# Mixing the two softmax maps two places behind the logits instead of one, with a deeper second buffer, in the second attention stage

## The reference

```python
def diff_mixer(h, rel_bias, w_in, lam_q1, ..., w_out, lambda_init):
    ...
    def block(args):
        ...
        logits = jnp.einsum('bqmd,blmd->bmql', qb, k).astype(jnp.float32)
        logits = logits + jnp.moveaxis(bias, -1, 0)[None]
        logits = jnp.where((rel >= 0)[None, None], logits, -jnp.inf)
        p = jax.nn.softmax(logits, axis=-1).reshape(bsz, B_HEADS, 2, BLOCK_Q, L)
        a = p[:, :, 0] - lam * p[:, :, 1]
        return jnp.einsum('bhql,blhe->bqhe', a.astype(v.dtype), v)
    ...
    o = rms_norm(o, subln_g) * (1.0 - lambda_init)
    return (o * jax.nn.silu(gate)) @ w_out
```

## Time and profile before

| | |
|---|---|
| median of 3 runs | 3884.29 us (3883.88 to 3887.35) |
| the profiled execution, its own time | 3887.83 us |
| its span | 3886.0 us |
| PE busy | 3448.4 us, 89% |
| DVE busy | 2143.9 us, 55% |
| ACT busy | 2016.0 us, 52% |
| GpSimd busy | 524.2 us, 13% |

### The profile page before, as it was taken

One profiled execution on the slowest core, in us unless ns is written; L12 is line 12 of the kernel. 1 busy time (PEld: TensorE's weight loads), 2 busy tenths in 40 slices (PEclk: granted clock), 3 DMA queues, 4 the chain that ended last, 5 costly groups with the idle time before them and its releaser, 6 DMA issues. The chain is left out here.

```text
span 3886.0 us, 65323 instructions
## 1 busy us (share of the span) xinstructions
PE 3448.4 (89%) x18786; PEld 2575.8 (66%) x18786; DVE 2143.9 (55%) x5870; ACT 2016.0 (52%) x3490; POOL 524.2 (13%) x550
## 2 busy tenths in 40 slices
PE   6869798878999999996975999999978899889699
PEld 3746454466666666664855888889956666666587
DVE  3659799995555556554644111000077777777344
ACT  2548689965777777774224111111156666666222
POOL 2000255101111111110211111111020000000011
PEclk7989899977999999998987999999989999999799
DMA  8651677663233222324532444322142222220342
GB/s 231 181 135 33 194 224 230 182 211 103 80 83 81 79 75 81 83 76 138 173 135 93 117 122 118 92 70 68 57 127 69 72 69 72 69 69 30 134 140 98
DMA packets 428415, 436.41 MB, mean 112 GB/s; under 512 B 81697, under 2 KB 341185, under 8 KB 427457
## 3 DMA queue, kind: packets, MB, share of 16 engines
q1 hardware_dynamic: 417440, 430.93, 37.4%
q10 hardware_dynamic: 10784, 3.18, 0.8%
HBM read 271.44 MB, written 162.53 MB: 112 GB/s over the span
## 5 line engine op out<-in xcount | busy, mean ns | idle before, releaser
L1253 DVE CUSTOM_DVE_ANT_0 a_att_sb_lg<-a_att_ps_s,mask 128x512 f32<-128x512 f32 (+3 forms) x512 | 302.0, 595 | 220.5 <-PE a_att_ps_s L1144 179.6
L1150 PE MATMUL b_att_ps_s<-b_att_sb_k,b_att_sb_q 64*128 64x512 f32 (+3 forms) x1920 | 295.2, 418 | 84.7 <-DVE b_att_sb_lg L1255 64.0
L1327 ACT ACTIVATE a_att_sb_pT<-a_att_ps_t 128x512 f32<-128x512 f32 (+3 forms) x640 | 316.0, 530 | 104.2 <-PE a_att_ps_t L1163 97.3
L1319 ACT ACTIVATE b_att_sb_lg<-b_att_sb_lg,b_att_sb_negm 128x384 f32<-128x384 f32 (+15 forms) x256 | 305.6, 1198 | 122.6 <-DVE b_att_sb_negm L1261 122.5
L1319 ACT ACTIVATE a_att_sb_lg<-a_att_sb_lg,a_att_sb_negm 128x384 f32<-128x384 f32 (+15 forms) x256 | 307.3, 1200 | 77.5 <-DVE a_att_sb_negm L1261 77.5
L1163 PE MATMUL a_att_ps_t<-ident,a_att_sb_lg 128*128 128x128 f32 x2176 | 339.8, 279 | 0.0
L1255 DVE TENSOR_SCALAR_CACHE_REDUCE b_att_sb_lg<-b_att_ps_s 128x512 f32<-128x512 f32 (+3 forms) x512 | 282.8, 590 | 95.8 <-PE b_att_ps_s L1150 80.4
L1682 DVE TENSOR_SCALAR_CACHE_REDUCE mask<-scores,threshold_bits 128x384 bf16<-128x384 f32 (+8 forms) x288 | 322.5, 1186 | 1.2
L1163 PEld LDWEIGHTS a_att_ps_t<-ident,a_att_sb_lg 128*128 128x128 f32 x2176 | 248.6, 141 | 107.4 <-issue 57.2
L1143 PE MATMUL a_att_ps_s<-a_att_sb_k,a_att_sb_q 128*128 128x512 f32 (+3 forms) x640 | 287.1, 449 | 30.9 <-DVE a_att_sb_mx L1253 16.4
L1180 PE MATMUL a_att_ps_o<-a_att_sb_pT,a_att_sb_v 128*64 128x256 f32 (+1 forms) x2304 | 297.4, 377 | 0.0
(11 more groups left out here) (282 smaller groups left out, 6896.4 us busy)
## 6 DMA issues: line engine op xcount, KB each, us to landing
a_att_sb_q<-scratch_qT SPq DMA_DIRECT2D x512, 64.0 KB, 2.5
select_sb_w_gate<-in_a_w_in SPq DMA_DIRECT2D x32, 512.0 KB, 4.9
mask_sb_mod_w<-in_mod_w SPq DMA_DIRECT2D x16, 1024.0 KB, 6.6
a_att_sb_k<-scratch_kT SPq DMA_DIRECT2D x128, 128.0 KB, 2.8
b_qkgv_sb_w<-in_b_w_in SPq DMA_DIRECT2D x32, 512.0 KB, 4.8
b_att_sb_q<-scratch_qT SPq DMA_DIRECT2D x128, 128.0 KB, 2.5
b_att_sb_k<-scratch_kT SPq DMA_DIRECT2D x64, 256.0 KB, 4.0
front_sb_mod_w<-in_mod_w SPq DMA_DIRECT2D x8, 1024.0 KB, 8.5
```

The lines of the kernel that those rows point to most:

```text
L1150: mm = nc.tensor.matmul(s_ps[:, (n + m) % SR, 0:z - a], q[rows, p // 2 % QS, x, cols], k[rows, slot, y, a:z], start=(j == 0), stop=(j == 2))
L1253: x = nc.vector.tensor_tensor_reduce(out, src, tab, 1.0, 2 * NEG, sign, ALU.max, top[:, col:col + 1])
L1319: nc.scalar.activation(buf, buf, ACT.Exp, bias=negm[:, p, m:m + 1], accum_out=sums[:, b, ds(h * M + m, 1)]).then_inc(exp_done, 1)
L1327: nc.scalar.activation(pT[:, r % 2, a:z, c:c + P], t_ps[:, n % TR, 0:z - a], ACT.Copy).then_inc(t_left, 1)
```

## The change

Four numbers and one test are different. DVE inverts and mixes block p - 2 at place p instead of block p - 1; `lg2` gets four buffers instead of two, which hold a block's second map for longer; and GpSimd prepares three early weight blocks instead of five, so that the last stage loads and splits five itself.

```diff
-EARLY_OUT = 5
+EARLY_OUT = 3
 OR = 2
 QS, OS, KPIECES = 4, 4, 4
-LR, LR2 = 4, 2
+LR, LR2 = 4, 4
...
                 if M == 2:
                     for head, x in both(h, p, before):
-                        if 1 <= x <= NB:
-                            invert(head, x - 1)
+                        if 2 <= x <= NB + 1:
+                            invert(head, x - 2)
                 if h is not None:
                     maximum(h, p)
                 for head, x in both(h, p, before):
                     for r in outputs_here(x):
                         output(head, r)
-                    if M == 2 and 1 <= x <= NB:
-                        mix(head, x - 1)
+                    if M == 2 and 2 <= x <= NB + 1:
+                        mix(head, x - 2)
```

## The result

Medians of four runs each: 3933.09 us after (3930.13 to 3936.11) against 3884.09 us before, a ratio of 1.0121 with a 95% interval of 1.0106 to 1.0136, or 49 us. 3922 was predicted, with a range of 3892 to 3960.

A forecast was written before the change was run, and what follows sets the result against it. DVE was taken to bound each head's growing part and PE the shrinking part; 25 (later mix) + 12 (clock) + 2.5 - 1.5 (early weights) = 38 us over the median of 3884.3, so 3922 us, range 3892 to 3960.

The forecast's parts named there:

- The mechanism: Second attention stage, growing part: transposes wait for the later mix, logits queue behind them, and DVE idles without PE's lead.
- two waits of 6.4 us for a mix: Kernel before: the transposes on PE were said to wait twice for a mix, 6.4 us in total.
- The main term, 25 us: Growing parts of the second attention stage: PE 3.1 us late per head by place 7, eight heads, +25 us.
- a barer loop end: DVE before place 6: a shorter mix covers less of the hardware loop's end, 0.41 us more per head.
- DVE's relief: Growing part: DVE mixes smaller blocks up to place 8, a gain of 1.87 us per head.
- The clock, 12 us: Growing parts: slow turns at 1.2 GHz now on DVE's path, 1.5 us per head, +12 us; ends 0 and 47.
- my own count: DVE's new idle at full clock: 0.34 us at a first wait, 0.26 for each further pair with transposes between.
- Rival 3: The clock stays low: all seven turns of a head at 1.2 GHz, 47 us instead of 12, 3957 us; 18%.
- Early weights: Two more ACT copies at the last stage's start, +2.5 us; less GpSimd work in the first head, -1.5 us.
- the lock rule: First head: DVE and GpSimd share a port lock for whole instructions; the saving could reach 9.5 us.
- Rival 1: The deferral wins: transposes come later than counted, only DVE's 1.87 us per head remains, 3870 us; 9%.
- Rival 2: The waits take each other's place: PE's new wait replaces 8 us per head of slot waits, 3885 us; 8%.

The follow-up runs named there:

- rest: Kernel before with three early weight blocks and four buffers for the second map, the mix left one place behind; ratio 0.9994.
- lead: Changed kernel with PE issuing the logits of chunk i + 1 ahead of the transposes of group i, at all places; 3889.57 us, ratio 1.0009.
- lead_before: Kernel before with PE's logits of chunk 1 and later issued ahead of the transposes at all places; 3904.69 us, ratio 1.0045.
- clean pair: Kernel before and changed kernel, each with DVE's loop cut between place 15 and place 0 (cut16, after_cut16); ratios 0.9959 and 1.0085.
- cut16: Kernel before with DVE's hardware loop in the second attention stage cut between place 15 and place 0, not before place 6; 3872.77 us, ratio 0.9959.
- after_cut16: Changed kernel with DVE's hardware loop cut between place 15 and place 0 instead of before place 6; ratio 1.0085.
- lead56: Changed kernel with PE's logits issued ahead of the transposes at places 5 and 6 only; 3912.56 us, ratio 1.0060.
- combo: Changed kernel with PE's logits ahead of the transposes at places 0 to 9 and DVE's loop cut between place 15 and place 0; 3855.98 us, ratio 0.9920.
- mid: Changed kernel with invert and mix of block p - 2 moved from the end of place p to right behind its first chunk pair; ratio 1.0076.
- lead9: Changed kernel with PE's logits issued ahead of the transposes at places 0 to 9 only, DVE's loop where it was; ratio 0.9968.

## Why the prediction was right, and what was mis-sized

**The mechanism** was as told. The mix a place later makes the transposes wait (predicted 30 to 70 us and some 60 times, measured 75.1 and 58), DVE loses its lead, PE's slot waits shrink, and `invert`'s wait (9.7 to 2.6) is worth nothing. That nothing else of the change matters is shown by `rest`. That the loss hangs on the order of transposes and logits on PE's queue is shown by `lead`, with `lead_before` as its control. That the logits queued behind the wait carry it, rather than the wait itself, is the reading of the rows above; in `lead` both went. The prediction's own start, two waits of 6.4 us for a mix, was a misreading of PE's loop end, and nothing in its sum hangs on it.

**The main term, 25 us**, was too small, and partly for wrong reasons. By place, from the clean pair: places 3 and 4 predicted 0.68 us of new idle time, measured 1.3; places 7 to 10 predicted 2.58, measured 2.7. Place 6 was put at nothing because the loop's end would hide it, with 0.41 for a barer loop end; `cut16` and `after_cut16` put the loop's end at about the same price in both kernels, so the 0.41 was about nothing and place 6 had a loss of its own. DVE's relief between the maxima of places 2 and 10 is the mix of 1664 keys less that of 384, 1.95 - 0.62 = 1.33 us, not 1.87; the rest of it falls where PE is the bound.

**The clock, 12 us, can't be told apart from the count.** The 25 and 12 us together should have been 48.5. In places 5 and 6 of the clean pair the new idle time is 3.8 us. At full clock my own count gives 0.60 for place 5 and, for place 6 without a loop's end, 0.86. The other 2.3 us, 18 in eight heads, are the most that slow turns can have added, an estimate. In places 3 and 4, where the changed kernel of the pair had the full clock (1.00), the same count was short by nearly half; if it is as short at places 5 and 6, about 1.1 us are left for the clock, 9 in eight heads. So the 12 us were too small, or were right while the count was too small; no run parts the two. `lead56` fits either: places 5 and 6 cost 3.8 x 8 = 30 us by this head, and the new order at these two places gave 24 back.

Two things were missed all the same. In the fourth head both groups of place 5 and the matmuls between them are slow, 1.96 us of wait and then 1.11, 1.65 and 0.90 in a row. And the low stretches grew: (1 - 0.95) x 2 x 772 = 77 us of the stage at 1.2 GHz before, (1 - 0.92) x 2 x 819 = 131 after. The same six matmuls take 1.65 us there and 0.97 at full clock, so the 54 us more can have cost at most 54 x (1 - 0.97 / 1.65) = 22, an estimate that takes PE as busy all the time. The clock of the growing part of the fourth head went from 0.93 to 0.84, while in `combo`, where PE idles 54.7 us in the growing parts instead of 102.8, the stage is at 0.98. The Trainium skill, page "TensorE: Matmul & The Clock Gate", section "A second HAM failure mode: psum-queue depth-cycling", describes such a swing between the two clocks for a bf16 kernel whose PE pauses briefly and often between groups of matmuls. These clocks agree with it. Rival 3, 47 us for the clock, did not come about: the last head lost 3.2 us with its clock no lower than before (0.94 against 0.93).

**Early weights.** Predicted +2.5 at the last stage's start and -1.5 in the first head. ACT at the start of the last stage, to be read against the earlier trace rows:

```profile
3644.64 0.38 ACT L1336 ACTIVATE b_att_sb_o_sb<-b_att_ps_o 128x256 f32<-128x256 f32 x1 [0.42 <-PE b_att_ps_o L1183]
3651.33 1.06 ACT L2089 ACTIVATE b_out_sb_w_hi<-b_out_sb_w 128x1024 fp32r<-128x1024 f32 x1 [6.31 <-DMA b_out_sb_w<-in_b_w_out]
3663.50 1.06 ACT L2089 ACTIVATE b_out_sb_w_hi<-b_out_sb_w 128x1024 fp32r<-128x1024 f32 x1 [11.11 <-DMA b_out_sb_w<-in_b_w_out]
...
3667.30 1.06 ACT L2089 ACTIVATE b_out_sb_w_hi<-b_out_sb_w 128x1024 fp32r<-128x1024 f32 x1 [0.19 <-DMA b_out_sb_w<-in_b_w_out]
3668.26 2.17 ACT L2054 ACTIVATE b_out_sb_hsq<-b_out_sb_o 128x512 f32<-128x512 f32 x4
```

Five copies, as said. From the last attention output to the squares it is 23.6 us, against 22.1 before (3620.92 - 3598.78): +1.5, since one block lands early and its copy hides in the wait. In `rest` the same stretch is 25.8, +3.6, though a block lands early there too; why the two differ is not shown. The first head's saving is not to be seen: `rest` has 55.27 us for its growing part against 55.14, and DVE is busy 52.67 us in it against 53.22. So neither the 1.5 us nor the 9.5 us that the lock rule would have allowed came in `rest`. The four operations that went measured 8.9 us (20.27 - 11.36) and not 9.5.

**The rivals.** Rival 1 fell by the queue order, not by the late mix alone: `lead` has DVE's mixes just as late and no loss. Rival 2's exchange of waits took place on PE (40 us of slot waits gone), but didn't protect DVE.

**Left open**: where two thirds of `mid`'s loss come from, though its transposes don't wait; how much of the loss at places 5 and 6 is the clock's; what a wait of the transposes costs with nothing queued behind it; and how much of the gain of `lead` and `combo` over their controls is the later mix's and how much the early weights'.

## What to carry to other kernels

Before a step is moved later on one engine, list what is queued in order behind its consumer on the other engine. If the margin is short, first put the independent work ahead of the waiting consumer; then the move can even pay (`lead9`, `combo`). Cut a hardware loop where its engine has slack and the next engine has work in hand, and look for the loop ends of all engines before an idle stretch is put down to a wait or to the clock. And before two totals of a wait list are compared, see that they hold the same waits.

## What the runs showed of the hardware

- The end of a hardware loop leaves its engine idle, where the loop branches back. On DVE it is 1.55 us in the earlier trace rows. At the same point of the changed kernel it is 4.38, and none of that is PE's lateness: the pair that DVE read next was in PSUM by 3157.55 (the matmuls of 2.93 us at 3154.62), and the profile calls the wait issue. Ahead of place 12 it is 2.77. The kernel before has six such branches, in the second to the seventh head, with 15 us of idle time in all; at the last head, where the loop is left, there is none. Moved to a place with slack, they saved 16 us of 3884. No group of instructions shows this cost, as the profile books it as a wait for PE or as issue.
- On PE the same pause was 2.94 and 3.31 us in `combo` and 3.26 us in the kernel before, in the two heads where its loop branches back. The profile books it as a wait for DVE. In `combo` it made these two heads about 3 us longer than the others, and the granted clock fell behind it.
